# Stick-breaking heads of a hybrid block: who adds the later key blocks, on which column halves the value products run, and another starting order

## What is computed

```
def stick_breaking_attention(q, k, v):        # q, k, v: 8 heads, 512 tokens, 64 wide
    ...
        z = jnp.einsum('bhqd,bhkd->bhqk', q_i, k) * scale
        mask = kpos[None, :] < qpos[:, None]
        log_fail = jnp.where(mask, jax.nn.log_sigmoid(-z), 0.0)
        later = lax.cumsum(log_fail, axis=3, reverse=True) - log_fail
        a = jnp.where(mask, jnp.exp(jax.nn.log_sigmoid(z) + later), 0.0)
        return jnp.einsum('bhqk,bhkd->bhqd', a, v)
```

## Time and profile before

| | us |
|---|---|
| median of 3 runs | 2915.82 (2915.56 to 2921.53) |
| the profiled execution | 2914.18, its span 2912.0 |
| hybrid mixer, first slab product to the first product of its output projection | 41.2 to 447.9 of the span |
| of that, up to the last slab product | 41.2 to 359.8 |
| PE busy over the span | 2796.6 (96%) |

### The profile page before, as it was taken

The page is one execution under the profiler, slowest core; times in us unless marked ns, Lnnn a source line. Parts: engine busy times, 40 slices in busy tenths (PEclk is TensorE's granted clock), DMA queues, the critical chain, the costliest instruction groups (busy, mean ns, idle before and its releaser), DMA issues.

```text
span 2912.0 us, 33354 instructions
## 1 busy us (share of the span) xinstructions
PE 2796.6 (96%) x13978; PEld 2244.8 (77%) x13978; DVE 1410.5 (48%) x2076; ACT 964.0 (33%) x1278; POOL 533.2 (18%) x414
## 2 busy tenths in 40 slices
PE   7998989999999999999999999899999998999998
PEld 4776657888887888888888877688888875788886
DVE  6645546666544333373222455555345365454453
ACT  3435444322233322243222333432223244332222
POOL 2563301100112201221001100012012100021121
PEclk9999989999999999999999999999999999999999
DMA  6322103456332222222632322122322311222321
GB/s 240 123 88 92 54 8 145 174 183 222 139 100 92 91 85 79 76 87 100 172 116 70 119 81 81 40 101 86 108 101 74 115 58 66 73 93 76 114 83 69
DMA packets 51093, 296.36 MB, mean 102 GB/s; under 512 B 6617, under 2 KB 6745, under 8 KB 25088
## 3 DMA queue, kind: packets, MB, share of 16 engines
q1 hardware_dynamic: 44912, 276.58, 27.1%
q0 software_dynamic: 4736, 15.34, 2.0%
q10 hardware_dynamic: 1296, 2.32, 0.2%
HBM read 283.46 MB, written 8.65 MB: 100 GB/s over the span
## 4 chain that ended last, share of the span: by engine, by line
PE 88%; DVE 5%; ACT 4%; issue 1%; POOL 1%; DMA 0%; SPq 0%; DVEq 0%
PE ps L218 88%; DVE wlo L211 1%; PE ps L1312 1%; ACT whi L200 1%; DMA F<-in_ada 0%; ACT F L1329 0%; DVE F L412 0%; DVE hl L416 0%; DVE ada L460 0%; DVE F L2260 0%; ACT L253 0%; ACT E L2833 0%; DVE F L827 0%; ACT E L2831 0%; ACT hh L430 0%
## 5 line engine op out<-in xcount | busy, mean ns | idle before, releaser
L218 PE MATMUL ps<-hh,whi 128*128 128x512 f32 x2088 | 829.6, 397 | 12.4 <-ACT F L2811 5.8
L218 PE MATMUL ps<-hl,whi 128*128 128x512 f32 x2088 | 815.4, 391 | 0.0
L218 PE MATMUL ps<-hh,wlo 128*128 128x512 f32 x2088 | 814.6, 390 | 0.0
L211 DVE TENSOR_TENSOR wlo<-raw,whi 128x2048 fp32r<-128x2048 f32 (+2 forms) x235 | 497.3, 2116 | 509.3 <-ACT whi L200 509.2
L218 PE MATMUL ps<-R,whi 128*128 128x512 f32 x2080 | 650.0, 391 | 8.0 <-DVE wlo L211 3.1
L200 ACT ACTIVATE whi<-raw 128x2048 fp32r<-128x2048 f32 (+2 forms) x235 | 409.6, 1743 | 686.2 <-PE ps L218 681.7
L218 PEld LDWEIGHTS ps<-hh,whi 128*128 128x128 f32 x2088 | 393.1, 188 | 103.7 <-issue 12.2
L218 PEld LDWEIGHTS ps<-R,whi 128*128 128x128 f32 x2080 | 390.5, 188 | 95.3 <-issue 6.9
L218 PEld LDWEIGHTS ps<-hl,whi 128*128 128x128 f32 x2088 | 393.0, 188 | 83.2
L218 PEld LDWEIGHTS ps<-hh,wlo 128*128 128x128 f32 x2088 | 393.4, 188 | 82.2 <-issue 3.3
L218 PE MATMUL ps<-R,wlo 128*128 128x512 f32 x1040 | 404.7, 389 | 0.0
(11 more groups left out here) (343 smaller groups left out, 2587.5 us busy)
## 6 DMA issues: line engine op xcount, KB each, us to landing
F<-in_ada SPq DMA_DIRECT2D x32, 1024.0 KB, 4.9
raw<-in_fs0in SPq DMA_DIRECT2D x22, 1024.0 KB, 6.1
raw<-in_fs1in SPq DMA_DIRECT2D x22, 1024.0 KB, 4.8
raw<-in_fc0in SPq DMA_DIRECT2D x22, 1024.0 KB, 4.9
raw<-in_fc1in SPq DMA_DIRECT2D x22, 1024.0 KB, 4.8
Rf<-in_ada0h SPq DMA_DIRECT2D x24, 512.0 KB, 3.5
raw<-in_fs0out SPq DMA_DIRECT2D x16, 704.0 KB, 4.5
raw<-in_fs1out SPq DMA_DIRECT2D x16, 704.0 KB, 4.1
```

The lines of the kernel that those rows point to most:

```text
L211: e.tensor_tensor(m.wlo[n % 2][:, 0:size], m.raw[m.slot[n]][:, 0:size], m.whi[n % 2][:, 0:size].bitcast(F32), SUB).then_inc(*s.up("wlo", n))
L218: return e.matmul(out, l, r, start=start, stop=stop, skip_group_check=True)
```

## The change

Three things are changed.

1. **Suffix sums.** PE makes for block c only the triangle product and one product with `ones`, on block c+1. Before that, DVE adds block c+1 (in which the still later blocks have been added already) to the later queries of block c, in place, as soon as the triangle product of c has read them (`sb_own`, `sb_later`). c runs 3, 2, 1, 0. It is 7 matmuls and 2048 columns instead of 10 and 2560.
2. **Values.** Blocks 1 and 2 are summed in the 64 partitions of bank 5 where all four were, blocks 0 and 3 in the other 64. ACT copies that other half to `E` (`sb_outer`), DVE adds the first half to it (`sb_o`), and the upper part and the rest are then made from `E`. The next head's first score waits for `sb_o`, the softplus of the next head for `sb_lo`.
3. **Order.** `heads` has 14 steps a head instead of 12, with other lengths; `FIRST_CHOICE` and `BEGIN` differ, and `delta1` may begin at 70 instead of 20.

```diff
-        for work in ("act:3.9", "dve:1.7", "pe:2.2"):
+        for work in ("act:3.9", "dve:1.7"):
             yield step(work)
-        yield step("pe:1.3", ("six", "sb_sub", h, 1), "dve:1.3")
-        yield step("pe:0.7")
-        yield step("pe:0.3 dve:0.7", ("six", "sb_sub", h, 3))
+        yield step("pe:0.3", ("six", "sb_sub", h, 3), "dve:0.3")
+        yield step("pe:0.7", beside="dve:1")
+        yield step("pe:1.1", ("six", "sb_sub", h, 1), "dve:0.4")
+        yield step("pe:1.5 dve:0.7", beside="dve:0.5")
...
-FIRST_CHOICE = ("gates", "heads", "delta0", "delta1", "ada", "stick")
-BEGIN = {"gates": 1.0, "ada": 13.0, "heads": 1.0, "delta1": 20.0, "delta0": 0.0, "stick": 1.0}
+FIRST_CHOICE = ("delta1", "heads", "ada", "delta0", "gates", "stick")
+BEGIN = {"gates": 1.0, "ada": 13.0, "heads": 1.0, "delta1": 70.0, "delta0": 0.0, "stick": 1.0}
...
             s.wait_ge("sb_sp", h)
-            for c in range(4):
+            for c in (3, 2, 1, 0):
                 if c % 2:
                     six_free(s, "sb_sub", h, c)
                 elif c:
-                    s.wait_ge("sb_sub", h, 0)
+                    s.wait_ge("sb_z", h, 2)
                 else:
-                    s.wait_ge("sb_z", h, 2)
-                for j in range(c, 4):
-                    w = T - j * P
-                    t = mm(e, m.ps[5 + c % 2][:, T - c * P - w:T - c * P], m.k("tril" if j == c else "ones"), stick_sp(m, j), j == c, j == 3)
+                    s.wait_ge("sb_sub", h, 2)
+                t = mm(e, m.ps[5 + c % 2][:, 0:T - c * P], m.k("tril"), stick_sp(m, c), True, c == 3)
+                if c < 3:
+                    t.then_inc(*s.up("sb_own", h, c))
+                    if c < 2:
+                        s.wait_ge("sb_later", h, c + 1)
+                    t = mm(e, m.ps[5 + c % 2][:, P:T - c * P], m.k("ones"), stick_sp(m, c + 1), False, True)
                 t.then_inc(*s.up("sb_cum", h, c))
                 yield
...
             for c in range(4):
-                t = mm(e, m.ps[5][rows, c * P:], v[:, c, 64 * h:64 * h + 64], stick_z(m, c), c == 0, c == 3)
+                half = rows if c in (1, 2) else swapped
+                t = mm(e, m.ps[5][half, c * P:], v[:, c, 64 * h:64 * h + 64], stick_z(m, c), c < 2, c > 1)
             t.then_inc(*s.up("sb_pv", h))
...
             s.wait_ge("sb_pv", h)
+            e.activation(stick_o(m, rows), m.ps[5][slice(64 - 64 * hh, 128 - 64 * hh), :], ACT.Copy).then_inc(*s.up("sb_outer", h))
+            yield from steps(2)
             if p == 3:
                 s.wait_ge("pw", 3)
-            e.activation(m.o(4 + p)[0][rows, :], m.ps[5][rows, :], ACT.Copy).then_inc(*s.up("sb_hi", h))
+            s.wait_ge("sb_o", h)
+            e.activation(m.o(4 + p)[0][rows, :], stick_o(m, rows), ACT.Copy).then_inc(*s.up("sb_hi", h))
...
-            for c in range(4):
-                s.wait_ge("sb_cum", h, c)
-                a = stick_z(m, c)
-                e.tensor_tensor(a, a, m.ps[5 + c % 2][:, 0:T - c * P], SUB).then_inc(*s.up("sb_sub", h, c))
+            for c in (2, 1):
+                s.wait_ge("sb_own", h, c)
                 if c == 1:
-                    yield from steps(2)
+                    s.wait_ge("sb_later", h, 2)
+                a = stick_sp(m, c)[:, P:]
+                e.tensor_tensor(a, a, stick_sp(m, c + 1), ADD).then_inc(*s.up("sb_later", h, c))
+                for i in (c + 1, c) if c == 2 else ():
+                    dve_stick_sub(e, s, m, h, i)
+                yield
+            for c in (1, 0):
+                dve_stick_sub(e, s, m, h, c)
```

More of the change, by code:

```diff
@@ L2717, in stick_sp, with stick_o @@
     return m.E[:, H_SP:H_SP + 1280] if c is None else m.E[:, H_SP + SOFF[c]:H_SP + SOFF[c] + T - c * P]
+def stick_o(m, rows):
+    return m.E[rows, H_SP:H_SP + T]
 def pe_stick(e, s, m):
@@ L2888, in dve_stick_heads @@
             yield from steps(2)
-            for c in range(4):
-                s.wait_ge("sb_cum", h, c)
-                a = stick_z(m, c)
-                e.tensor_tensor(a, a, m.ps[5 + c % 2][:, 0:T - c * P], SUB).then_inc(*s.up("sb_sub", h, c))
+            for c in (2, 1):
+                s.wait_ge("sb_own", h, c)
                 if c == 1:
-                    yield from steps(2)
+                    s.wait_ge("sb_later", h, 2)
[6 more added lines that the diff above has]
+                dve_stick_sub(e, s, m, h, c)
             yield from steps(4)
             hi, lo = m.o(4 + p)
+            o = stick_o(m, rows)
+            s.wait_ge("sb_outer", h)
+            e.tensor_tensor(o[:, P:], o[:, P:], m.ps[5][rows, P:], ADD).then_inc(*s.up("sb_o", h))
+            yield from steps(2)
             s.wait_ge("sb_hi", h)
-            e.tensor_tensor(lo[rows, :], m.ps[5][rows, :], hi[rows, :].bitcast(F32), SUB).then_inc(*s.up("sb_lo", h))
+            e.tensor_tensor(lo[rows, :], o, hi[rows, :].bitcast(F32), SUB).then_inc(*s.up("sb_lo", h))
             yield
```

29 lines of the change are left out of this document (18 added, 11 removed).

## The result

The changed kernel takes 2924.36 us (median of 18 executions, 2916.9 to 2931.67), the kernel before 2915.69 (18, 2911.79 to 2924.92): ratio 1.0031, interval 1.0022 to 1.0041. Slower by 0.2% or more was given 0.08. The predicted 2902 is 22 us off and the range ends 10 us short.

A forecast was written before the change was run, and what follows sets the result against it. PE's work was taken to bound the mixer until 359.8 us, then the chain of heads 6 and 7. Heads -11.8 and -1.6, Order (c) -2, (a) +2, (b) +1: -12.4 from 2914.18, say 2902; range 2891 to 2914.

The forecast's parts named there:

- The bound: Mixer: PE work removed counts fully before 359.8 us, afterwards only by its share of a head's latency.
- Suffix sums, -7.0: Heads' suffix sums on PE: 512 columns fewer a head, 0.87 us each, 7.0 us for eight, called certain.
- Value products, -8.7: Heads' value products on two column halves: full overlap assumed, 1.09 us less a head, 8.7 us in all.
- program order: Rival on value products: column halves start and end in program order, 3 us less gain, 2905 us; chance 0.10.
- DVE +10, ACT +4.7, hidden: Added DVE additions (10 us) and ACT copies (4.7 us) in the heads: beside PE's work before 359.8, costing nothing there.
- (a): Changes between slab products and others on PE: 113 instead of 99, 0.1 to 0.2 us each, +2 us.
- (b): Slab borders: stall after `sbqk` 1 goes, 5 to 6 us after `sbqk` 2, about 2 after `sbqk` 0; together +1.
- Order (c): Last slab product comes earlier: about 4 us of PE products move behind it, half hidden in idle time there.
- Order (d): `delta1` later, heads 0 to 5 earlier: effect on mixer idle time taken as 0, with 8 us either way.
- The order takes back what PE saves: Rival: 6 us more idle at head 7 and `sbqk` borders, some 3 us of half clock, 2911 us; chance 0.15.
- POOL comes late: Rival: POOL's last `ada` batch delays PE if products take over 12.3 us; at 12.5 us, 2922 us; chance 0.07.
- No overlap: Rival on value products: column halves do not overlap, the 8.7 us are missing, 2910 to 2911 us; chance 0.08.

The follow-up runs named there:

- e4: Kernel before with only the suffix sums changed, old step order but for two moved steps: 2920.7 us, ratio 1.0024.
- e5: e4 with the smallest triangle product issued five times, giving back 512 columns a head: 2924.1 us, ratio 1.0030 to the kernel before.
- e1: Changed kernel with the step order of the kernel before (two steps moved slightly): 2919.5 us, ratio 1.0003 to the kernel before.
- e11: Changed kernel with both planner inputs of the kernel before (first choice, `delta1` at 20), order made anew: 2915.9 us, ratio .9996 to the kernel before.
- e2: Kernel before with the step order of the changed kernel: 2929.4 us, ratio 1.0045.
- e14: e4 with ACT's copies of slab `sbqk` 1 moved ahead of head 1's passes: 2918.5 us, ratio 1.0009 to the kernel before.

## Why the prediction was wrong, point by point

**The bound** was read off an average. "A microsecond of PE work taken away counts fully before 359.8" is the step that failed. PE is busy 92% there, but the other 8% are waits for other chains, and the products that went stood partly in front of points whose time another chain sets (3.6 us at 200, 2.5 us at 320, with or without them). e4 shows a loss where 7.0 us of gain were counted, e5 shows 7 us of given-back work costing half or less in its central values. In the sum: heads' code was to give 13.4 us and e1 has +0.9; the order was to cost 1 and costs 8.

**Suffix sums, -7.0.** The products went, but the term should have been a cost of about 5.7 us. Its miss is 13 us, as large as the whole forecast gain. The +0.4 us of latency a head left out that the first group shrinks from 1280 columns to 128. It was asked whether PE waits for the second addition, and not who had needed the first group as cover. The additions were under-priced too. Groups by line on DVE, all of the mixer:

```profile
L2915 DVE TENSOR_TENSOR E<-E 128x128 f32<-128x128 f32 x8 | 4.7, 592 | 10.6 <-PE ps L218 10.6
L2915 DVE TENSOR_TENSOR E<-E 128x256 f32<-128x256 f32 x8 | 4.2, 529 | 11.6 <-PE ps L218 11.6
```

I had taken 0.29 and 0.42 us from subtractions that read PSUM; between two SBUF operands these took 0.59 and 0.53 in the mean, 0.41 us more a head for the two. The means hide that twelve of the sixteen took just the predicted 0.29 and 0.42 to 0.43 us; the other four (0.54, 1.40, 1.34 and, of the wide ones, 1.26) are the four that overlapped a POOL instruction. Not every overlap does it: in e4 two beside POOL took 0.33 and 0.43. The second addition, priced at nothing, ended no wait of PE in after (one of 1.88 us in e11, at 283.77). What PE did wait for are the subtractions that free bank 6, `DVE E L2889`: 4.9 us in five places, which no term of the sum had.

**Value products, -8.7.** The mechanism was right and nearly exact in the trace: 1.06 us a head of 1.09, full overlap. The rule of program order in the Trainium skill ("TensorE: Matmul & The Clock Gate", section "Part 3: Packing small matmuls — row/col tiling") would have given about 1.5 us for the group; the trace has 1.23 from start to next start, so for these two-record float32 products the rule's reading in the prediction isn't borne out. The single records say so too: in the group at 359.72 block 1's second record starts at 360.10, ahead of block 0's second at 360.18. In time the four comparisons give 5.7 us instead of 8.7, two thirds. That the rest goes to waits as with the sums is likely and not shown; with some 2 us to a side the difference is hardly beyond noise.

**DVE +10, ACT +4.7, hidden.** DVE's new additions come to 4.7 + 4.2 + 4.4 = 13.3 us by the groups (the last is the 64x384 one, 0.55 us each), ACT's as priced. They lie beside PE's work in sum. That some stand between PE's groups is part of the sums' cost above.

**Order (a) and (b), +2 and +1.** The stall after `sbqk` 1 went, and one of 5 to 6 us after `sbqk` 2 came: 5.59. Right, and the same 5.59 in e2 shows that it belongs to the order. Behind `sbqk` 0 it was 1.04 us (at 128.74) where 2 had been put. What the changes of kind in (a) cost was not measured. But a further border, free before, costs 4.12 us at 339.36. And passes of a head stand in front of a copy for a delta chain (`ACT F L2533`, 4.33 us of wait at 377.85). The prediction looked at the `sbqk` borders alone.

**Order (c).** The work behind the last slab product grew, from 529 products to 751, and that tail is 1.5 us longer, not shorter. The last slab product came at 362.8 where "13 to 17 shorter" was the sign of being right.

**Order (d), idle time taken as 0 with 8 us either way.** This is the term that failed beside the sums: the idle time rose by 15.0 us, almost twice the allowance, 11.0 of them ahead of the last slab product. The order alone costs 8 to 13 us (after against e1, e2 against before). I had seen the planner's order as neutral in the mean. The four orders made from changed inputs lie 3.5 to 9 us above the one of the kernel before, and the fifth (e11) is level. None of the orders made from other inputs was better than the one of the kernel before.

**The clock** stood in the prediction as a note on the tail and in none of its terms. It is 24 us more at the lower level in the mixer. Fitting the start of the projection over all seventeen profiled executions gives -2.9 us with the sums (e5, which has its work back, counted as without), -8.0 with the value halves, +0.50 per us of wait and +0.36 per us at the lower clock, with 1.1 us left over (rms). For after against before that is -2.9 - 8.0 + 0.50 x 15.0 + 0.36 x 23.9 = +5.2, measured +4.8. This is a description and no proof of cause; waits and lower clock come together and no run here changed one without the other. That the clock falls after waits is seen in rows: `raw,Rf` 1.16 us and 2.00 behind 1.19 and 3.11 us of wait, yet 1.16 in e14 behind 3.12. So a wait does not always bring it on. The Trainium skill says in the same page, section "Part 1: The HAM clock gate (the "warmup" mystery)", that the default state is throttled and that activity releases it. The rows agree with the direction. How much of it an execution gets differs between executions of one kernel here (0.978 to 0.984 in after), and most of their 15 us of scatter goes with it.

**Rivals.** Two happened at once. "The order takes back what PE saves" named the right mechanism with its price too low (6 us of idle time and 3 at the lower clock, where 15.0 and 24 came). The wait behind head 7's scores that it describes is the 5.39 us at 443.22. ACT's three passes for head 7 start as soon as the scores are through, DVE's softplus follows, and PE has nothing left; the timelines of ACT and DVE:

```profile
437.68 1.27 ACT L2843 ACTIVATE E<-E 128x1280 f32<-128x1280 f32 x1
...
441.68 1.49 DVE L2908 SCALAR_TENSOR_TENSOR E<-E 128x1280 f32<-128x1280 f32 x1 [4.03 <-ACT E L2847]
```

 "POOL comes late" happened at another batch than the one computed: 4.26 us at 97.50, because PE has no `delta1` work in front of it; it was worked out for the last batches only. "No overlap" and "program order" did not happen. The tail from head 6's first scores (402.68) to the projection is 50.1 us, as forecast (at most 55); the last value products stand at 451.5, not 434.

**What stays open.** The profiles show 2.7 of the 8.7 us between the medians; the rest lies in executions with a lower mean clock than the profiled one, and no profile here is of one of those. Why e1 falls into two groups 12 us apart, one at each of two mean clocks, is not settled. Nor was it tried to begin the ladder of sums with a wide group, so that this would mend it is not shown.

## What to carry to other kernels

Products that are removed from a busy engine give time only where nothing else fixes the end of the stretch; before counting them, look at the timeline for who is waiting while they run, and for the wait that they would leave behind. Where a chain hands over to a slower engine, a wide first group can be the cover for it; ask this before making it small. A changed planner input is a new order with waits of its own: measure old code in new order and new code in old order before crediting either, and look first for single steps whose queue place makes the longest wait; in the old order moving one of them was worth as much as the value halves, in two other orders the same kind of move gave nothing or a loss, so it has to be measured in the order at hand.

## What the hardware showed that I had not expected

Two products on different column halves of the array, with moving rows of the same partitions, overlap fully: 640 + 640 columns in 1.23 us against 2.29 in a row. A DVE addition of 128x128 between SBUF operands took 0.59 us in the mean of eight, longer than the 0.53 of one twice as wide; but five of the eight took 0.29, and the slow ones, up to 1.40 us, all ran beside a POOL instruction. A mean of a group hides this. And with identical instructions one kernel's executions spread over 15 us out of 2924 with the mean clock (0.978 to 0.984), more than any of the single changes tested here is worth.
